# Operand tiles with a home of their own in each stage, 0 to 192 bytes further on

## The chip, the cores and the metric

The kernel runs as one program on one core of a Trainium2 chip. The metric is the device time of one execution in microseconds (us). Two executions of the kernel before took 2618.04 and 2622.47 us, median 2620.26 us.

## The reference, cut to what matters

The program computes two small networks one after the other, all in float32, on 256 tokens of width 1024.

```python
# first block: two layers on x (256 latents) and ctx (256 context tokens)
x = x + 0.5 * gt1 * swiglu(modulate(x, g1, sh1, sc1), ffn1_wi[i], ffn1_wo[i])   # same for ctx
y = conformer_conv(...)          if i == 0      # pointwise, 31 taps, LayerNorm, pointwise
y = windowed_gqa_sink(...)       if i == 1
x = x + gt2 * y
x = x + 0.5 * gt3 * swiglu(modulate(x, g3, sh3, sc3), ffn2_wi[i], ffn2_wo[i])
x = rmsnorm(x, final_g)
# second block: two layers on x alone
h = h + mixer_ab(rms(h)) or mixer_nsa(rms(h))   # attention
h = h + swiglu(rms(h), w_ffn_gate, w_ffn_up, w_ffn_down)                        # hidden 2816
h = h + sigmoid(rms(h) @ w_ple_gate) * (p[i] @ w_ple_proj)
```

Nearly all the arithmetic is products of a weight matrix with 1024 or 2816 rows by a few hundred token columns: six feed-forward layers, the projections around the convolution and around three attentions, and the modulation vectors `silu(c) @ ada_w`. Their weights are read once.

## The kernel before, in words

**A weight slab.** The weights come from HBM in slabs of 1 MB: 128 partitions by 2048 floats, which are 8 tiles in k (128 input rows each) of 256 output columns. The sync engine loads them in turn into two slots of `raw`. ScalarE rounds a slab to float32r in `whi` (line 774), VectorE takes the remainder `raw - whi` in `wlo` (line 1308), each in halves of 1024 floats.

**An operand tile.** The tokens stand on the free axis: `hhi[p, k, t]` is the rounded normalised activation of channel `128 k + p` of token `t`, `hlo` its remainder. Both are `[128, 8, 512]` float32r. Their writers are the norm stages, the convolution and, for a late norm, the residual stage ahead of it. `ghi` and `glo` are the same for the 2816 gated channels, `[128, 22, 512]`; `ohi` and `olo`, `[128, 8, 256]`, hold the output of an attention.

**A product.** `split_mm` (lines 1853 to 1857) makes three matmuls for each tile of 128 output rows: `whi` by `hi`, `whi` by `lo`, `wlo` by `hi`. In each the 128x128 weight tile is loaded into the array (a LDWEIGHTS of its own in the trace, engine PEld) and the 512 or 256 token columns of the operand are streamed through it. `tiles_of` runs it over the 8 k tiles and 2 output tiles of a slab: 48 matmuls. So the moving operand is always one row of an operand tile, and the weight tile of the next matmul is loaded while this one streams. `tokens_of` and `value_step` turn that round: `hhi` is loaded as the weights and `whi` streams.

**The stages**, in the order of the program: three feed-forward layers on 512 columns (`up`, 22 slabs, then `down`, 12 slabs, which reads `ghi` and `glo`), of which between the first and the second stand `pw1` (8 slabs, 512 columns), the convolution on TensorE, ScalarE and VectorE, and `pw2` (4 slabs, 512 columns). In the three `up` stages the matmuls of the modulation (line 1932, 32 columns of weights) stand between the slabs. Then on 256 columns: `qkv` (its fifth slab on 512), attention, `wo` (4 slabs, reads `ohi`), `up`, `down`; `qknorm` (8 slabs), attention, `wo`, `up`, `down`, `pleproj`, `plegate` (4 slabs); `nsa` (11 slabs), attention, `wo`, `up`, `down`, `pleproj`, `plegate`.

**What sets the order.** Each engine has its own program, written out by hand from a plan of stages, with counting semaphores between them. The trace's lines of interest: 1855 to 1857 (the three matmuls), 774 and 1308 (the split of the slab), 1392, 1399 and 1517 (`hlo`), 1932 (modulation), 1907 to 1909 and 2283 to 2285 (`hhi` as weights).

**Where the tiles lie.** The tiles are laid out in the order in which they are declared. In bytes of a partition, and past the last multiple of 256:

| tile | start, before | past 256, before |
|---|---|---|
| `hhi` / `hlo` | 32896 / 49280 | 128 / 128 |
| `whi` / `wlo` | 82048 / 98432 | 128 / 128 |
| `ghi` / `glo` | 136000 / 181056 | 64 / 64 |
| `ohi` / `olo` | 136000 / 144192 | 64 / 64 |
| `uhi` / `ulo` (convolution, moving) | 195264 / 202144 | 192 / 160 |
| `diag_hi` / `diag_lo` (convolution, weights) | 170688 / 182976 | 192 / 192 |

A row of an operand tile is 2048 bytes, a weight tile 512 bytes in a row of 1024, so within a stage the remainders of 256 are the same for every k tile.

Of the kernel before, what the change touches and what calls it, by code (L numbers as in the profile page):

```python
# [21 lines left out]
P = 128  # L22
# [107 lines left out]
class Stage:  # L130


    def __init__(self, kind, slabs=0, T=S, mod=None, layer=0, ada=0, gate=None, how=None, gain=None, what=None):
        self.kind, self.slabs, self.T, self.mod, self.layer = kind, slabs, T, mod, layer
        self.ada, self.gate, self.how, self.gain, self.what = ada, gate, how, gain, what
        self.late, self.feeds, self.norm, self.both, self.direct = False, None, None, False, False
        self.next_norm, self.carried = None, False


def ffn_stages(layer, tokens, ada=0, mod=None):  # L140

    return [Stage("up", 22, T=tokens, ada=ada), Stage("down", 12, T=tokens, mod=mod)]


def make_plan():
# [45 lines left out]
    for i, norm in enumerate(st):  # L191
        if norm.kind == "norm" and st[i - 1].kind == "plegate":
            st[i - 1].next_norm, norm.carried = norm, True
        if norm.kind == "norm" and not norm.late:
            j = i - 1
            while st[j].kind == "mods":
                j -= 1
            if st[j].kind in ("down", "pw2", "wo"):

                st[j].direct = norm.direct = True  # L200
                st[j:i] = st[j + 1:i] + [st[j]]
    return st

# [119 lines left out]
def build(nc, slabs_d, x_d, vec_d, const_d, w2_d, tab_d, hot_d, rope_d, mask_d, p_d, out_d, stop_after=None):  # L323
# [10 lines left out]
    with ExitStack() as ctx:  # L334
# [53 lines left out]
        with ExitStack() as at:  # L388
# [30 lines left out]
        phi, plo = hhi[:, 0:2, S:2 * S], hlo[:, 0:2, S:2 * S]  # L419
        pp = x[:, :, S:2 * S]  # L420
# [103 lines left out]

        block = ctx.enter_context(nc.Block())

        def x_final(eng, st):
# [231 lines left out]
        def _(act):  # L759
# [74 lines left out]
            def up_late(st):  # L834
                n, m = st.n0, st.m0
                with act.Fori(0, 11) as i:

# [9 lines left out]
            def up(st):  # L847
                if st.late:
                    up_late(st)
                    return  # L850
                both = st.ada // 2
                act.wait_ge(lines_done, 16)
                for first, count, ada in ((0, both, True), (both, 11 - both, False)):
# [21 lines left out]
            def residual(st):  # L875
                ks = st.slabs // 4

                def last_squares(m):
# [50 lines left out]
            def norm(st):  # L929
# [5 lines left out]
                if not st.summed:  # L935
                    preload(ACT.Sqrt)
                x_final(act, st)
                if st is not opening:
# [83 lines left out]
            def conv(st):  # L1022

                x_final(act, st)
                u_high(6)
# [231 lines left out]

            def pleload(st):
                act.wait_ge(p_landed, 16 * (st.layer + 1))
                nc.scalar.activation(phi, ptok[:, :, :], ACT.Copy).then_inc(p_split, 1)  # L1260
# [37 lines left out]
        def _(dve):  # L1298
# [73 lines left out]
            def norm(st):  # L1372
                if st.late:
                    inverse(st)
                    return
                x_final(dve, st)
                if st is not opening:
                    inverse(st)
# [39 lines left out]
            def up_late(st):  # L1418
                n, m = st.n0, st.m0
                a, b = acc[:, m % 2, :, 0:S], acc[:, (m + 1) % 2, :, 0:S]  # L1420
                scale = across(rs[:, 0:S], 2)
                dve.wait_ge(rs_ready, st.rs0)
                with dve.Fori(0, 11) as i:
# [18 lines left out]
            def up(st):  # L1442
                if st.late:
                    up_late(st)
                    return
                both = st.ada // 2
                for first, count, ada in ((0, both, True), (both, 11 - both, False)):
                    if not count:
# [19 lines left out]
            def residual(st):  # L1468

                ks = st.slabs // 4  # L1470
                xf = x[:, :, :].rearrange("p a b -> p (a b)")
                mGf = mG[:, :, :, :].rearrange("p a b c -> p (a b c)")
# [107 lines left out]
            def conv(st):  # L1580

                u_low(6)
                u_low(7)
# [237 lines left out]

            def pleload(st):
                dve.wait_ge(p_split, 2 * st.layer + 1)
                nc.vector.tensor_tensor(plo, ptok[:, :, :], phi.bitcast(F32), ALU.subtract).then_inc(p_split, 1)
# [27 lines left out]
        def _(pe):  # L1852
# [18 lines left out]
            def tiles_of(n, m, op, T, i=0, per=0, k0=0, nk=SLAB_K, first=True, last=True, paced=None,  # L1871
                         mid=None, operand=None):


                for k in range(nk):
# [5 lines left out]
                    if paced:  # L1881
                        pe.wait_ge(h_ready, paced.h0 - paced.made + paced.made * (k + 1) // DT)
                    if operand and k0 + k in operand[1]:
                        pe.wait_ge(operand[0], operand[1][k0 + k])
                    for t in range(2):
# [5 lines left out]

            def tokens_of(n, m, count, cols=SLAB_N, i=0, per=0, behind_first=None):

                for tt in range(count):
                    if tt == 1 and behind_first:
# [127 lines left out]
            def half_pair(st, c, n, m, i, per):  # L2023

                slab_there(n, i, per)
                set_free(m, i, 2)
                tiles_of(n, m, (hhi, hlo), st.T, i, per, paced=st if c == 0 else None).then_inc(slab_used, 1)

            def up_late(st):
                n, m = st.n0, st.m0  # L2030
                slab_there(n)
                set_free(m)
                tiles_of(n, m, (hhi, hlo), S, paced=st, mid=st.norm).then_inc(slab_used, 1)
                half_pair(st, 1, n + 1, m + 1, 0, 2)
                with pe.Fori(0, 10) as i:
                    for c in range(2):
                        slab_there(n + 2 + c, i, 2)
                        set_free(m + 2 + c, i, 2)
                        tiles_of(n + 2 + c, m + c, (hhi, hlo), S, i, 2).then_inc(slab_used, 1)

# [33 lines left out]
            def residual(st):  # L2074
                ks = st.slabs // 4
                operand = None
                if st.kind == "down":
                    op, operand = (ghi, glo), (g_lo, {0: st.g0, HT - 2: st.g0 + 1})
                elif st.kind == "wo":
                    made = 2 + 8 * st.att0  # L2080
                    op, operand = (ohi, olo), (o_lo, {0: made - 1, DT - 1: made})
                else:
                    op = (hhi, hlo)
                with pe.Fori(0, 2) as i:
                    for c in range(2):
                        m = st.m0 + c
                        set_free(m, i, 2)
                        for kk in range(ks):
# [4 lines left out]
                                     paced=st if st.kind == "pw2" and c == 0 else None,  # L2093
                                     operand=operand if c == 0 else None).then_inc(slab_used, 1)

# [32 lines left out]
            def qkv(st):  # L2128
# [8 lines left out]
                for c in range(6):  # L2137
# [3 lines left out]
                    if c < 5:  # L2141
                        ins = tiles_of(n, m, (hhi, hlo), S if c < 4 else 2 * S, paced=st if c == 0 else None)
                    else:
                        ins = tokens_of(n, m, 4, behind_first=lambda: rotated(4))
                    ins.then_inc(slab_used, 1)
# [3 lines left out]
            def qknorm(st):  # L2149
                n, m = st.n0, st.m0  # L2150
                with pe.Fori(0, st.slabs // 2) as i:
                    for c in range(2):
                        slab_there(n + c, i, 2)
                        set_free(m + c, i, 2)
                        tiles_of(n + c, m + c, (hhi, hlo), S, i, 2, paced=None if c else st).then_inc(slab_used, 1)
                    for c in range(2):
# [5 lines left out]
            def nsa(st):  # L2162
# [6 lines left out]
                def tiles(p):  # L2169
                    there(p)  # L2170
                    tiles_of(n + p, m + p, (hhi, hlo), S, paced=st if p == CK else None).then_inc(slab_used, 1)

# [6 lines left out]
                def hidden(kv):  # L2179
                    pe.wait_ge(mlp_landed[kv], 16)  # L2180
                    pe.wait_ge(cmp_dve, kv + 1)
                    for k in range(16):
                        ins = nc.tensor.matmul(B[3 * kv][:, 0:64], mlp[:, kv, P * k:P * k + P], blk[:, kv, k, :],
                                               start=(k == 0), stop=(k == 15))
                    ins.then_inc(hid_done, 1)

                def gate_tiles():
# [35 lines left out]
                there(V0)  # L2223
                tokens_of(n + V0, m + V0, 2).then_inc(slab_used, 1)
                pe.wait_ge(cmp_dve, 4)
# [18 lines left out]
                there(V1)  # L2244
                tokens_of(n + V1, m + V1, 2).then_inc(slab_used, 1)

            def att(st):
                A0 = 32 * st.att0
                win, nsa = st.what == "window", st.what == "nsa"
                ab = st.what == "ab"  # L2250
                if ab:
                    x_final(pe, st)
# [124 lines left out]
            def pleproj(st):  # L2377

                pe.wait_ge(p_split, 2 * st.layer + 2)
                slab_there(st.n0)  # L2380
# [12 lines left out]
            def plegate(st):  # L2393
                for c in range(4):
                    slab_there(st.n0 + c)
                    set_free(st.m0 + c)
                    tiles_of(st.n0 + c, st.m0 + c, (hhi, hlo), S, paced=None if c else st).then_inc(slab_used, 1)
                    if st.next_norm and c:
# [124 lines left out]
```

## Time and profile before

| | |
|---|---|
| two executions | 2618.04 and 2622.47 us, median 2620.26 |
| the profiled execution, first to last instruction | 2621.3 us |
| TensorE matmul busy | 2505.4 us, 96% |
| TensorE weight load busy | 2139.4 us, 82% |
| VectorE busy | 1336.2 us, 51% |
| ScalarE busy | 1155.1 us, 44% |
| mean granted TensorE clock | 0.973 |
| data moved | 374.88 MB, 143 GB/s |

The profiled execution has no time of its own beside the span; its span lies between the two times and 1.0 us above their median. Busy is the union of the recorded lengths. The length of a matmul in the trace (389 ns) is longer than the distance to the next one (227 ns), since matmuls are pipelined; what a matmul costs a stream is the distance from start to start.

### The profile page before, as it was taken

Reading aid. Unit: us, or ns where it says so; the run is one execution under the profiler, and the core shown is the slowest. Engines: PE = TensorE matmul, PEld = TensorE weight load, DVE = VectorE, ACT = ScalarE, POOL = GpSimd, SP = SyncE. Lnnn points to the kernel's source line nnn. Section 1 sums busy time; section 2 is a strip of 40 time slices with the busy share of each in tenths; the row PEclk is TensorE's granted clock in tenths of the full one; section 3 lists DMA queues with packets and bytes.
Section 4 is the critical chain, followed back from the end, with each engine's and each line's share of the span. In section 5 each row is a group of like instructions: output and inputs, shape, how many; then the busy total and the mean of one; then the engine's idle time right before and its main releaser. Section 6 shows DMA issues by size and latency. Waiting matters only on the chain.

```text
span 2621.3 us, 39926 instructions
## 1 busy us (share of the span) xinstructions
PE 2505.4 (96%) x15799; PEld 2139.4 (82%) x15799; DVE 1336.2 (51%) x2003; ACT 1155.1 (44%) x1827; POOL 23.7 (1%) x37
## 2 busy tenths in 40 slices
PE   6999999998999999999999998999889998979998
PEld 4777787875777778777788777999869998869998
DVE  4323334896523233422333466555777665776665
ACT  3323323464433322332322356554556555565554
POOL 0000000000000000000000000000100001000000
PEclk8999999999999999999999999999999998999999
DMA  7444542210344442244423221445424455403554
GB/s 312 167 161 170 186 172 88 89 49 1 114 181 170 161 159 96 104 185 160 170 102 112 82 96 65 176 176 193 166 79 177 180 194 196 157 34 116 189 188 150
DMA packets 52724, 374.88 MB, mean 143 GB/s; under 512 B 5822, under 2 KB 7034, under 8 KB 8736
## 3 DMA queue, kind: packets, MB, share of 16 engines
q1 hardware_dynamic: 50000, 358.63, 37.0%
q0 software_dynamic: 2208, 14.37, 1.6%
q8 instruction: 55, 0.90, 0.1%
q10 hardware_dynamic: 432, 0.73, 0.1%
q14 instruction: 29, 0.24, 0.0%
HBM read 372.55 MB, written 7.39 MB: 145 GB/s over the span
## 4 chain that ended last, share of the span: by engine, by line
PE 89%; DVE 6%; ACT 2%; issue 1%; DMA 1%; SPq 0%; ACTq 0%; DVEq 0%
PE acc L1855 27%; PE acc L1856 26%; PE acc L1857 26%; PE bank L1932 3%; DVE wlo L1308 1%; PE bank L1959 1%; DMA ada_raw<-in_slabs 1%; PE acc L2352 1%; DVE prod L598 1%; DVE sc L1757 1%; PE acc L2326 1%; PE bank L1990 1%; DVE prod L1674 0%; PE Mod L1942 0%; DVE hlo L1392 0%
## 5 line engine op out<-in xcount | busy, mean ns | idle before, releaser
L1308 DVE TENSOR_TENSOR wlo<-raw,whi 128x1024 fp32r<-128x1024 f32 x534 | 646.0, 1223 | 901.4 <-ACT whi L774 900.9
L774 ACT ACTIVATE whi<-raw 128x1024 fp32r<-128x1024 f32 x534 | 556.2, 1055 | 969.8 <-PE acc L1857 912.5
L1855 PE MATMUL acc<-hhi,whi 128*128 128x256 f32 (+1 forms) x2808 | 949.1, 338 | 30.0 <-DVE hlo L1392 13.2
L1856 PE MATMUL acc<-hlo,whi 128*128 128x256 f32 (+1 forms) x2808 | 935.2, 333 | 0.0
L1857 PE MATMUL acc<-hhi,wlo 128*128 128x256 f32 (+1 forms) x2808 | 934.9, 333 | 0.0
L1855 PEld LDWEIGHTS acc<-hhi,whi 128*128 128x128 f32 x2808 | 538.8, 192 | 115.0 <-issue 58.6
L1857 PEld LDWEIGHTS acc<-hhi,wlo 128*128 128x128 f32 x2808 | 538.7, 192 | 50.3
L1856 PEld LDWEIGHTS acc<-hlo,whi 128*128 128x128 f32 x2808 | 539.2, 192 | 49.7 <-issue 1.7
L1855 PE MATMUL acc<-ghi,whi 128*128 128x512 f32 (+1 forms) x1056 | 354.5, 336 | 0.0
L1856 PE MATMUL acc<-glo,whi 128*128 128x512 f32 (+1 forms) x1056 | 354.3, 336 | 0.0
L1857 PE MATMUL acc<-ghi,wlo 128*128 128x512 f32 (+1 forms) x1056 | 354.3, 336 | 0.0
L1855 PEld LDWEIGHTS acc<-ghi,whi 128*128 128x128 f32 x1056 | 198.2, 188 | 24.1
L1857 PEld LDWEIGHTS acc<-ghi,wlo 128*128 128x128 f32 x1056 | 198.2, 188 | 24.0
L1856 PEld LDWEIGHTS acc<-glo,whi 128*128 128x128 f32 x1056 | 198.2, 188 | 24.0
L1460 DVE TENSOR_TENSOR prod<-gate_sb,acc 128x1024 f32<-128x1024 f32 (+1 forms) x44 | 47.9, 1088 | 111.8 <-PE acc L1857 111.8
L1543 DVE SCALAR_TENSOR_TENSOR v<-ubuf,vec,v 128x512 f32<-128x512 f32 x150 | 100.0, 757 | 0.0
L1932 PE MATMUL bank<-raw,cwin 128*32 128x256 f32 x992 | 69.0, 398 | 1.1 <-issue 1.1
L958 ACT ACTIVATE hhi<-prod,mB 128x256 fp32r<-128x256 f32 x88 | 43.2, 506 | 35.6 <-DVE prod L598 35.5
L1855 PE MATMUL acc<-ohi,whi 128*128 128x256 f32 x192 | 54.5, 284 | 0.3 <-DVE olo L1792 0.3
L1856 PE MATMUL acc<-olo,whi 128*128 128x256 f32 x192 | 54.2, 282 | 0.0
L860 ACT ACT_TABLE_LOAD x42 | 53.9, 1283 | 0.7
L1857 PE MATMUL acc<-ohi,wlo 128*128 128x256 f32 x192 | 54.2, 282 | 0.0
(286 smaller groups left out, 2201.1 us busy)
## 6 DMA issues: line engine op xcount, KB each, us to landing
raw<-in_slabs SPq DMA_DIRECT2D x329, 1024.0 KB, 4.8
ada_raw<-in_slabs SPq DMA_DIRECT2D x10, 1024.0 KB, 26.1
skew_dram<-lines_dram POOLq DMA_DIRECT2D x1, 6144.0 KB, 23.7
bt<-skew_dram POOLq DMA_DIRECT2D x4, 1024.0 KB, 9.4
x<-in_x_in SPq DMA_DIRECT2D x1, 2048.0 KB, 17.8
mlp<-in_slabs POOLq DMA_DIRECT2D x2, 1024.0 KB, 6.1
out<-x SPq DMA_DIRECT2D x1, 1024.0 KB, 4.8
rope<-in_rope POOLq DMA_DIRECT2D x1, 512.0 KB, 4.0
```

The source lines that it names most:

```text
L598: return engine.scalar_tensor_tensor(dst, x[:, c, cols], g, r[:, cols], ALU.mult, ALU.mult)
L774: nc.scalar.activation(whi[:, n % 2, cols], raw_of(n, cols), ACT.Copy).then_inc(ready, 1)
L860: nc.scalar.activation(junk_act[:, :], eps[:, :], ACT.Silu)
L958: ins = nc.scalar.activation(dst, ub[:, k % 4, :], ACT.Identity, bias=mB[:, st.mod, c, s:s + 1])
L1308: nc.vector.tensor_tensor(wlo[:, n % 2, cols], raw_of(n, cols), whi[:, n % 2, cols].bitcast(F32), ALU.subtract).then_inc(low, 1)
L1460: nc.vector.tensor_tensor(prod[:, :, 0:T], gate_sb[:, :, 0:T], acc[:, (m + 1) % 2, :, 0:T], ALU.mult).then_inc(acc_free[(m + 1) % 2], 1)
L1543: nc.vector.scalar_tensor_tensor(tile, ub2[:, 2 * j:2 * j + 2, t:t + S], vec[:, w:w + 1], tile, ALU.mult, ALU.add).then_inc(conv_dve, 1)
L1757: ins = nc.vector.tensor_tensor_reduce(probs(st, v)[:, keys * s:keys * s + keys], B[v % 4][:, keys * s:keys * s + keys], bias, 1.0, LOWEST ...
L1855: nc.tensor.matmul(out, w[0], xx[0], start=first, stop=False)
L1856: nc.tensor.matmul(out, w[0], xx[1], start=False, stop=False)
L1857: return nc.tensor.matmul(out, w[1], xx[0], start=False, stop=last)
L1932: ins = nc.tensor.matmul(ada_bank(st, a // 2)[32 * j:32 * j + 32, 0:SLAB_N], cwin[:, k, at:at + 32], src[:, k * SLAB_N:(k + 1) * SLAB_N], ...
```

## The change: what it does

Each of `hhi`, `hlo`, `ghi` and `glo` becomes a flat buffer, 64 floats (256 bytes) longer for the first two and 32 floats (128 bytes) longer for the others. A stage sees its operand tile as a window in that buffer that begins at the stage's home. A home is a number of floats, a pair for (hi, lo) of `hhi` and `hlo`, one number for `ghi` and `glo`. The writer of an operand and its readers take the same home. Two small tiles, `kcsq` and `kcr`, give their room and become parts of `arow`.

```diff
+ROOM, G_ROOM = 64, 32
+HOMES = dict(up=((16, 16), (32, 32), (48, 48), (16, 16), (32, 32), (8, 8)), pw1=((8, 8),), conv=((0, 16),),
+             qkv=((16, 0),), qknorm=((8, 8),), plegate=((32, 32), (8, 8)), nsa=((48, 48),))
+G_HOMES = (16, 8, 32, 16, 8, 32)
+
+def place_operands(plan):
+    left = {kind: list(homes) for kind, homes in HOMES.items()}
+    home, g_home, ups = (0, 0), 0, 0
+    for i, st in enumerate(plan):
+        if st.kind in ("norm", "conv"):
+            reader = st.kind if st.kind == "conv" else plan[i + 1].kind
+            home = left[reader].pop(0)
+        if st.kind == "up":
+            g_home = G_HOMES[ups]
+            ups += 1
+        st.home, st.g_home = home, g_home
...
-        hhi = sb("hhi", [P, DT, 2 * S], F32R)
-        hlo = sb("hlo", [P, DT, 2 * S], F32R)
+        hhi_all = sb("hhi", [P, DT * 2 * S + ROOM], F32R)
+        hlo_all = sb("hlo", [P, DT * 2 * S + ROOM], F32R)
...
-            ghi = sb("ghi", [P, HT, 2 * S], F32R, ffn)
-            glo = sb("glo", [P, HT, 2 * S], F32R, ffn)
+            ghi_all = sb("ghi", [P, HT * 2 * S + G_ROOM], F32R, ffn)
+            glo_all = sb("glo", [P, HT * 2 * S + G_ROOM], F32R, ffn)
...
-            kcsq = sb("kcsq", [P, 64], F32, at)
-            kcr = sb("kcr", [P, 64], F32, at)
...
+        kcsq, kcr = arow[:, 0, 0:64], arow[:, 0, 64:128]
...
+        def operand(st):
+            return tuple(a[:, at:at + DT * 2 * S].rearrange("p (a t) -> p a t", t=2 * S)
+                         for a, at in zip((hhi_all, hlo_all), st.home))
...
+        def gated_operand(st):
+            return tuple(a[:, st.g_home:st.g_home + HT * 2 * S].rearrange("p (a t) -> p a t", t=2 * S)
+                         for a in (ghi_all, glo_all))
...
-                tiles_of(n, m, (hhi, hlo), st.T, i, per, paced=st if c == 0 else None).then_inc(slab_used, 1)
+                tiles_of(n, m, operand(st), st.T, i, per, paced=st if c == 0 else None).then_inc(slab_used, 1)
```

The homes that result, in bytes, in the order of the stages:

| stage (columns) | `hhi` | `hlo` | `ghi` and `glo` |
|---|---|---|---|
| first `up`, `down` (512) | 64 | 64 | 64 |
| `pw1` (512) | 32 | 32 | |
| `pw2` (512) | 0 | 64 | |
| second `up`, `down` (512) | 128 | 128 | 32 |
| third `up`, `down` (512) | 192 | 192 | 128 |
| `qkv` (256, one slab 512) | 64 | 0 | |
| fourth `up`, `down` (256) | 64 | 64 | 64 |
| `qknorm` (256) | 32 | 32 | |
| fifth `up`, `down`, `pleproj`, `plegate` (256) | 128 | 128 | 32 |
| `nsa` (256) | 192 | 192 | |
| sixth `up`, `down`, `pleproj`, `plegate` (256) | 32 | 32 | 128 |

With the longer buffers `hlo` starts 256 bytes later than before, `whi`, `wlo`, `ghi`, `ohi` and all that follows 512 bytes later, `glo` 640 bytes later. So against `whi` and `wlo`, modulo 256, `hhi`, `hlo` and `ghi` move by their home alone and `glo` by its home and 128; `ohi`, `olo` and the tiles of the convolution stay as they were. The instructions of each engine, their sizes, their order and their waits are the same as before, but for the names `kcsq` and `kcr`.

## Rows read from the trace of the kernel before

**Rows 1.** The page: busy by engine, granted clock in 40 slices, end chain.

```profile
PE 2505.4 (96%) x15799; PEld 2139.4 (82%) x15799; DVE 1336.2 (51%) x2003; ACT 1155.1 (44%) x1827; POOL 23.7 (1%) x37
...
PEclk8999999999999999999999999999999998999999
...
PE 89%; DVE 6%; ACT 2%; issue 1%; DMA 1%; SPq 0%; ACTq 0%; DVEq 0%
```

**Rows 2.** Groups by shape: names, count, busy us, mean ns, idle before.

```profile
L1855 PE MATMUL acc<-hhi,whi 128*128 128x512 f32 x1264 | 502.8, 398 | 17.5 <-DVE hlo L1601 7.4 <-DVE hlo L1392 6.6 <-issue 3.6
L1855 PE MATMUL acc<-hhi,whi 128*128 128x256 f32 x1544 | 446.3, 289 | 12.5 <-DVE hlo L1392 6.6 <-DVE hlo L1399 5.8
L1855 PE MATMUL acc<-ghi,whi 128*128 128x512 f32 x528 | 208.7, 395 | 0.0
L1855 PE MATMUL acc<-ghi,whi 128*128 128x256 f32 x528 | 145.8, 276 | 0.0
...
L1907 PE MATMUL acc<-whi,hhi 128*128 128x256 f32 x64 | 20.4, 318 | 0.8 <-DVE wlo L1308 0.8
```

**Rows 3.** Stretches by stage: span, PE, PEld, DVE, ACT, POOL, clock, DMA, GB/s.

```profile
452.00:541.00 89.00, 89.00 (x384) 73.27 (x383) 76.32 (x117) 45.11 (x91) 0.00 (x0) 0.97 0.27 95
...
1982.00:2109.00 127.00, 127.00 (x1057) 126.89 (x1057) 84.30 (x91) 78.67 (x94) 0.00 (x0) 1.00 0.51 186
2109.00:2169.00 60.00, 60.00 (x531) 60.00 (x530) 36.88 (x40) 28.51 (x34) 0.00 (x0) 1.00 0.53 202
2200.00:2276.00 76.00, 68.87 (x522) 65.86 (x521) 49.97 (x54) 45.39 (x72) 12.92 (x16) 0.91 0.50 180
...
2583.00:2621.00 38.00, 30.09 (x246) 29.46 (x245) 21.50 (x25) 16.70 (x22) 0.00 (x0) 0.95 0.31 111
```

**Rows 4.** TensorE in order of time, `hhi`, 512 columns: first and 28th.

```profile
299.85 0.39 PE L1855 MATMUL acc<-hhi,whi 128*128 128x512 f32 x1
...
305.97 0.39 PE L1855 MATMUL acc<-hhi,whi 128*128 128x512 f32 x1
```

**Rows 5.** The same, `ghi`, 512 columns: first and 19th.

```profile
323.63 0.39 PE L1856 MATMUL acc<-glo,whi 128*128 128x512 f32 x1
...
327.83 0.39 PE L1856 MATMUL acc<-glo,whi 128*128 128x512 f32 x1
```

**Rows 6.** The same, convolution, 512 columns: first and 27th.

```profile
569.83 0.40 PE L1855 MATMUL acc<-uhi,diag_hi 128*128 128x512 f32 x1
...
575.90 0.39 PE L1857 MATMUL acc<-uhi,diag_lo 128*128 128x512 f32 x1
```

**Rows 7.** The same, `hhi`, 256 columns: first and 19th.

```profile
1699.74 0.28 PE L1857 MATMUL acc<-hhi,wlo 128*128 128x256 f32 x1
...
1701.90 0.28 PE L1857 MATMUL acc<-hhi,wlo 128*128 128x256 f32 x1
```

**Rows 8.** The same, `ghi`, 256 columns: first and 20th.

```profile
1779.81 0.28 PE L1856 MATMUL acc<-glo,whi 128*128 128x256 f32 x1
...
1781.96 0.28 PE L1857 MATMUL acc<-ghi,wlo 128*128 128x256 f32 x1
```

**Rows 9.** The same, `ohi`, 256 columns: first and 20th.

```profile
1614.78 0.28 PE L1855 MATMUL acc<-ohi,whi 128*128 128x256 f32 x1
...
1616.94 0.28 PE L1856 MATMUL acc<-olo,whi 128*128 128x256 f32 x1
```

**Rows 10.** The same, `hhi`, 512 columns, at the half clock: first and fourth.

```profile
48.53 0.63 PE L1857 MATMUL acc<-hhi,wlo 128*128 128x512 f32 x1
...
49.81 0.63 PE L1857 MATMUL acc<-hhi,wlo 128*128 128x512 f32 x1
```

More of the change, by code:

```diff
@@ L835, in up_late @@
                 n, m = st.n0, st.m0
+                ghi, glo = gated_operand(st)
                 with act.Fori(0, 11) as i:
@@ L851, in up @@
                 both = st.ada // 2
+                ghi, glo = gated_operand(st)
                 act.wait_ge(lines_done, 16)
@@ L876, in residual @@
                 ks = st.slabs // 4
+                hhi, hlo = operand(st.feeds or st)
                 def last_squares(m):
@@ L936, in norm @@
                     preload(ACT.Sqrt)
+                hhi, hlo = operand(st)
                 x_final(act, st)
@@ L1022, in conv @@
             def conv(st):
+                hhi, hlo = operand(st)
                 x_final(act, st)
@@ L1376, in norm @@
                 x_final(dve, st)
+                hhi, hlo = operand(st)
                 if st is not opening:
@@ L1421, in up_late @@
                 scale = across(rs[:, 0:S], 2)
+                ghi, glo = gated_operand(st)
                 dve.wait_ge(rs_ready, st.rs0)
@@ L1446, in up @@
                 both = st.ada // 2
+                ghi, glo = gated_operand(st)
                 for first, count, ada in ((0, both, True), (both, 11 - both, False)):
@@ L1470, in residual @@
                 ks = st.slabs // 4
+                hhi, hlo = operand(st.feeds or st)
                 xf = x[:, :, :].rearrange("p a b -> p (a b)")
@@ L1580, in conv @@
             def conv(st):
+                hhi, hlo = operand(st)
                 u_low(6)
@@ L1890, in tiles_of, with tokens_of @@
                 return ins
-            def tokens_of(n, m, count, cols=SLAB_N, i=0, per=0, behind_first=None):
+            def tokens_of(n, m, op, count, cols=SLAB_N, i=0, per=0, behind_first=None):
+                hhi, hlo = op
                 for tt in range(count):
@@ L2032, in up_late @@
                 set_free(m)
-                tiles_of(n, m, (hhi, hlo), S, paced=st, mid=st.norm).then_inc(slab_used, 1)
+                tiles_of(n, m, operand(st), S, paced=st, mid=st.norm).then_inc(slab_used, 1)
                 half_pair(st, 1, n + 1, m + 1, 0, 2)
@@ L2038, in up_late @@
                         set_free(m + 2 + c, i, 2)
-                        tiles_of(n + 2 + c, m + c, (hhi, hlo), S, i, 2).then_inc(slab_used, 1)
+                        tiles_of(n + 2 + c, m + c, operand(st), S, i, 2).then_inc(slab_used, 1)
             def up(st):
@@ L2141, in qkv @@
                     if c < 5:
[L2142 removed]
+                        ins = tiles_of(n, m, operand(st), S if c < 4 else 2 * S, paced=st if c == 0 else None)
                     else:
[L2144 removed]
+                        ins = tokens_of(n, m, operand(st), 4, behind_first=lambda: rotated(4))
                     ins.then_inc(slab_used, 1)
@@ L2154, in qknorm @@
                         set_free(m + c, i, 2)
-                        tiles_of(n + c, m + c, (hhi, hlo), S, i, 2, paced=None if c else st).then_inc(slab_used, 1)
+                        tiles_of(n + c, m + c, operand(st), S, i, 2, paced=None if c else st).then_inc(slab_used, 1)
                     for c in range(2):
@@ L2170, in tiles @@
                     there(p)
-                    tiles_of(n + p, m + p, (hhi, hlo), S, paced=st if p == CK else None).then_inc(slab_used, 1)
+                    tiles_of(n + p, m + p, operand(st), S, paced=st if p == CK else None).then_inc(slab_used, 1)
                 def head_sums(p):
@@ L2185, in hidden @@
                     ins.then_inc(hid_done, 1)
+                hhi, hlo = operand(st)
                 def gate_tiles():
@@ L2250, in att @@
                 ab = st.what == "ab"
+                hhi, hlo = operand(st)
                 if ab:
@@ L2396, in plegate @@
                     set_free(st.m0 + c)
-                    tiles_of(st.n0 + c, st.m0 + c, (hhi, hlo), S, paced=None if c else st).then_inc(slab_used, 1)
+                    tiles_of(st.n0 + c, st.m0 + c, operand(st), S, paced=None if c else st).then_inc(slab_used, 1)
                     if st.next_norm and c:
```

29 lines of the change are left out of this document (18 added, 11 removed).

## The prediction

> **What bounds the kernel now.** I read the page first. TensorE is busy for 96% of the span, the chain that ended last runs through it for 89%, and the granted clock is full nearly everywhere [rows 1]. So the question is what one matmul costs in the stream. The change touches nothing but the place of its operand, and the groups by shape say how many there are: line 1855 is one of three equal lines, so `hhi` and `hlo` stream 3 x 1264 = 3792 times with 512 columns and 3 x 1544 = 4632 times with 256, `ghi` and `glo` 3 x 528 = 1584 times with each [rows 2]. The stretches by stage show that inside a stage nothing else limits: TensorE is busy for 89.00 of 89, 127.00 of 127 and 60.00 of 60 us while VectorE and ScalarE have room, though VectorE is at 76 of 89 us in `pw1` [rows 3].
>
> Then the starts in order of time give the price. From start to start:
>
> | operand, columns | rows | price, ns | columns at 2.4 GHz, ns | loss, ns | operand against weights, modulo 256 |
> |---|---|---|---|---|---|
> | `hhi`, 512 | [rows 4], 6.12 us / 27 | 226.7 | 213.3 | 13.4 | 0 bytes |
> | `ghi`, 512 | [rows 5], 4.20 us / 18 | 233.3 | 213.3 | 20.0 | 192 |
> | conv, 512 | [rows 6], 6.07 us / 26 | 233.5 | 213.3 | 20.2 | many (4 bytes per tap) |
> | `hhi`, 256 | [rows 7], 2.16 us / 18 | 120.0 | 106.7 | 13.3 | 0 |
> | `ghi`, 256 | [rows 8], 2.15 us / 19 | 113.2 | 106.7 | 6.5 | 192 |
> | `ohi`, 256 | [rows 9], 2.16 us / 19 | 113.7 | 106.7 | 7.0 | 192 |
>
> Same line, same shape, same clock, and the price differs by 6 to 7 ns with the tile that streams. That is what this change can move. The last column comes from the table of addresses: `hhi` lies 128 past a multiple of 256 as `whi` does, `ghi` and `ohi` 64 past. The sign is what I want the reader to see: being level with the weights is the better place at 512 columns and the worse one at 256. A further sign that weight load and stream disturb each other: at half clock the same matmul costs 1.28 us / 3 = 426.7 ns, which is 512 columns at 1.2 GHz with no loss at all [rows 10]. There the stream goes at half its full pace.
>
> **The change part by part.** No instruction, size or wait is added or removed, so each term is a count times a difference of two prices.
>
> *512 columns, moved whole.* The three `up` stages (22 slabs x 48 = 1056 each, 3168) and `pw1` (8 x 48 = 384) are 3552 matmuls. Their new distances are 64, 128, 192 and 32 bytes. One of them, 192, has a row (233.3); the convolution walks over many others and comes to 233.5, which is the nearest evidence for 32, 64 and 128. I take 233.3 for all: 3552 x 6.6 ns = +23.4 us. Bounds: 213.3 (no loss, as at half clock) and 240 (a loss once more as large over the level place).
>
> *512 columns, moved in part.* `pw2` moves only `hlo`, one matmul of three (64 of 192), and the one 512 slab of `qkv` only `hhi`, two of three (32 of 48): 96 x 6.6 ns = +0.6 us.
>
> *256 columns, moved whole.* Three `up` (3168), `qknorm` (384), the tile slabs of `nsa` (8.5 x 48 = 408), two `plegate` (384) and two `pleproj` (96) are 4440 matmuls, at distances 64, 32, 192, 128 and 32. Two rows off the level place give 113.2 and 113.7, both at 192, and no row tells of 32, 64 or 128. I take 113.3 for all, 6.7 ns less: -29.7 us. Bounds: 106.7 (no loss) and 126.7 (the loss grows by as much as it could fall).
>
> *256 columns, in part.* `qkv` moves two of three of 192: 128 x 6.7 = -0.9 us. `hhi` as weights (line 1907 and the two after it, 64 each [rows 2]) would win 192 x 6.7 = -1.3 us; the same in the attention of `mixer_ab` stands between waits and is taken at nothing.
>
> *What is lost of it.* In the stretch of `nsa` TensorE is busy for 68.87 of 76 us and in the last `plegate` for 30.09 of 38 [rows 3]: it waits there for steps that do not get shorter. I take half of the 408 + 192 matmuls as hidden: 300 x 6.7 = +2.0 us.
>
> *`ghi` and `glo`.* The new distances of (`ghi`, `glo`) are (0, 128), (224, 96) and (64, 192) bytes, once each with 512 and with 256 columns. Only the first makes two of three matmuls level: 352 x 6.6 ns less at 512 and 352 x 6.7 more at 256, which is 0. The others stay off level, 0.
>
> *The writers, the two small tiles, the slabs.* ScalarE and VectorE write at starts that remain multiples of 32 bytes, and TensorE waits for `hlo` only 26 us in all (7.4 + 6.6 + 6.6 + 5.8, lines 1601, 1392 and 1399 [rows 2]); 0. `kcsq` and `kcr` in `arow` have the waits that they had, 0. Faster 256-column slabs need faster slabs from HBM: 48 x 113.3 ns is 5.4 us each, and `down` takes 12 slabs in 60 us, 5.0 us each, with TensorE never idle [rows 3]. That cover holds.
>
> Sum: +23.4 + 0.6 - 29.7 - 0.9 - 1.3 + 2.0 = -5.9 us, against the profiled execution's 2621.3 us: 2615.4. That execution is 1.0 us over the median, so **2614 us**. The change is small because two tariffs nearly cancel, not because nothing happens.
>
> **A rule that speaks against it.** Prices at one shape differ by 6 to 7 ns between tiles [rows 7, 8]. The Trainium skill ("TensorE: Matmul & The Clock Gate", Part 2, step-by-step) says that TensorE has two independent read ports into SBUF and that loading the next weights takes no bandwidth from the running matmul, and gives N / 2.4 + 2.5 ns from start to start; by that every `hhi` matmul would cost 215.8 or 109.2 ns, at any address. This case's trace disagrees with the figures (226.7 and 120.0).
>
> **The rivals.**
>
> *1. Placement modulo 256 is not the cause.* The tiles that differ in price also differ in region: `hhi` lies below `whi`, while `ghi`, `ohi` and `uhi` lie above it. If region sets the price, or anything that 32 bytes do not change, nothing moves: 2620. For: no row has one tile at two places. Against: a loss that differs between 512 and 256 columns in opposite directions looks like two address streams meeting, and a far region has no reason to help one and harm the other. Beside this stands the Trainium skill ("SBUF — State Buffer", the box on cachelines): lines of 16 bytes and a price for crossing them. All homes are multiples of 32 bytes, so by that rule too the time stays at 2620.
>
> *2. Off level is better everywhere.* 192 may be the one bad distance at 512 columns, and the convolution's figure may come from its two-piece rows. Then 512-column matmuls fall to 220.0, by one step of 6.7: 3552 x -6.7 = -23.8; with -29.9 from the 256-column terms and `ghi` and `glo` at 226.7 instead of 233.3 with 512 columns (1584 x -6.6 = -10.5) the time is 2556. The milder form, 512 as it is and 256 lower, gives 2590. For: homes of 32 to 128 bytes are untried in the trace. Against: over 26 convolution matmuls at changing distances the mean is the 233.5 of the bad place.
>
> *3. The 512-column price rises and the 256-column one does not fall.* If only 192 bytes gives 113.3 at 256 columns, then of the moved stages `nsa` alone gains, some 1 us, and the rest stay at 120. With 512 columns at 233.3 that is +24 - 1: 2643; at 236 (9.3 ns over, 3552 of them) 2653. It decides from the point where the 256-column saving is under 24.0 / 4440 = 5.4 ns each. For: only one distance off level is priced at 256 columns. Against: nothing in the rows.
>
> **How the numbers follow.** Forecast 0.39, rival 1 0.19, rival 2 0.21 (a third of it in the strong form), rival 3 0.21. The forecast's own range is 2598 to 2630: a fifth of the moved matmuls in either class at the other price. To hold 8 in 10 the range takes in rival 1, the milder rival 2 (2590, with a little below it) and rival 3 up to 2648: **2580 to 2648**. Two per cent, about what a measurement can tell from no change, is 52 us here: 2568 and 2673. Faster by more needs the strong rival 2: 0.07. Slower by more needs rival 3 with the 256-column price up a step as well (+24 + 30 us): 0.04. Within: 0.89.
>
> **What the changed profile would show.** Start to start in the first three `up` stages: 233 if the term is right, 227 for rival 1, 220 or less for rival 2. In the fourth `up`: 113 if right, 120 for rivals 1 and 3. `nsa` at 113 is the surest number, for it has the distance of `ghi` before. In the first `down` two of three matmuls level with the weights should bring 233 towards 229, and in the fourth `down` 113 towards 118. `ohi` and the convolution must read as before. What would make it wrong: a price that depends on how far hi and lo lie from each other, or on the distance modulo 512, since `hlo` moved by 256 against `hhi` and the trace before never separated those; and waits at the ends of stages that grow when the matmuls get quicker.

## The result and the profile after

The changed kernel takes 2637.64 us (2637.38 and 2637.91) against 2620.26 before: ratio on record 1.0058, 95% interval 1.0037 to 1.008. The ratio makes it 15.2 us slower, the two medians 17.4 us (their quotient is 1.0066); with two executions of each kernel the two agree within the interval. That is inside the stated range of 2580 to 2648 and inside 2%, but above no change, where 2614 was forecast: the sign was wrong.

The page of the changed kernel, the lines that answer to [rows 1]:

```profile
span 2635.2 us, 39926 instructions
PE 2524.0 (96%) x15799; PEld 2143.7 (81%) x15799; DVE 1336.7 (51%) x2003; ACT 1155.8 (44%) x1827; POOL 23.7 (1%) x37
...
PE 89%; DVE 6%; ACT 2%; issue 1%; DMA 1%; SPq 0%; ACTq 0%; DVEq 0%
```

TensorE is busy 18.6 us longer, VectorE and ScalarE within 1 us as before. The groups by shape of the changed kernel (line 1855 is now 1903), to be held against [rows 2]:

```profile
L1903 PE MATMUL acc<-hhi,whi 128*128 128x512 f32 x1264 | 510.0, 404 | 15.1 <-DVE hlo L1648 7.4 <-DVE hlo L1435 4.2 <-DVE wlo L1350 3.6
L1903 PE MATMUL acc<-hhi,whi 128*128 128x256 f32 x1544 | 442.5, 287 | 12.8 <-DVE hlo L1435 6.7 <-DVE hlo L1442 5.8
```

The recorded 512-column matmul became longer (398 to 404 ns), the 256-column one shorter (289 to 287). The waits ahead of them moved little, from 17.5 to 15.1 us and from 12.5 to 12.8. By stage, the stretches that answer to [rows 3] (columns as there, ends cut at whole us):

```profile
454.00:546.00 92.00, 91.38 (x383) 72.82 (x384) 77.32 (x120) 45.85 (x92) 0.00 (x0) 0.98 0.26 92
...
2000.00:2126.00 126.00, 126.00 (x1061) 125.90 (x1060) 84.68 (x92) 79.01 (x94) 0.00 (x0) 1.00 0.53 186
2126.00:2188.00 62.00, 62.00 (x532) 62.00 (x532) 37.47 (x41) 28.52 (x34) 0.00 (x0) 1.00 0.54 199
```

`pw1` takes 92 us instead of 89, the fifth `up` 126 instead of 127, the fifth `down` 62 instead of 60; from first start to last they are 2.3 us longer, 1.4 shorter and 1.9 longer. Now the starts in order of time in the changed kernel, as in [rows 4] to [rows 9]. Each pair is the first and the last of 19 (first `up`) or 31 matmuls: `hhi` with 512 columns in the first `up` (home 64 bytes), `pw1` (32) and the third `up` (192).

```profile
102.22 0.39 PE L1903 MATMUL acc<-hhi,whi 128*128 128x512 f32 x1
...
106.34 0.39 PE L1903 MATMUL acc<-hhi,whi 128*128 128x512 f32 x1
...
469.66 0.40 PE L1904 MATMUL acc<-hlo,whi 128*128 128x512 f32 x1
...
476.66 0.40 PE L1904 MATMUL acc<-hlo,whi 128*128 128x512 f32 x1
...
1199.78 0.39 PE L1904 MATMUL acc<-hlo,whi 128*128 128x512 f32 x1
...
1206.78 0.39 PE L1904 MATMUL acc<-hlo,whi 128*128 128x512 f32 x1
```

4.12 / 18 = 228.9 ns, 7.00 / 30 = 233.3 and again 233.3, where 226.7 stood. With 256 columns: the fifth `up` (128 bytes), the sixth (32) and the fourth `down`.

```profile
2049.75 0.28 PE L1903 MATMUL acc<-hhi,whi 128*128 128x256 f32 x1
...
2053.31 0.28 PE L1903 MATMUL acc<-hhi,whi 128*128 128x256 f32 x1
...
2449.82 0.28 PE L1904 MATMUL acc<-hlo,whi 128*128 128x256 f32 x1
...
2453.32 0.28 PE L1904 MATMUL acc<-hlo,whi 128*128 128x256 f32 x1
...
1799.78 0.28 PE L1904 MATMUL acc<-glo,whi 128*128 128x256 f32 x1
...
1803.31 0.28 PE L1904 MATMUL acc<-glo,whi 128*128 128x256 f32 x1
```

118.7, 116.7 and 117.7 ns. The first two were 120.0 and were forecast at 113.3; the last was 113.3 before and was forecast to rise towards 118.

Below, a price is the mean over a whole stage of the distances from start to start under 140 ns (256 columns) or 260 ns (512). The lengths of the stages, from first start to last, add the difference up: 512-column `hhi` stages +16.7 us, 256-column `hhi` stages -8.4, `ghi` and `glo` -1.5 with 512 columns and +6.6 with 256; together +13.4 of the 13.9 us between the spans.

### The profile page after: what moved, and what is told of

It is laid out like the page before. It is cut to its first block, busy times and chain, and to the rows that moved or that the text cites. A ratio compares the mean times of both kernels' runs of the same rounds, so it can differ in the third digit from the quotient of the medians.

```text
span 2635.2 us, 39926 instructions
## 1 busy us (share of the span) xinstructions
PE 2524.0 (96%) x15799; PEld 2143.7 (81%) x15799; DVE 1336.7 (51%) x2003; ACT 1155.8 (44%) x1827; POOL 23.7 (1%) x37
## 4 chain that ended last, share of the span: by engine, by line
PE 89%; DVE 6%; ACT 2%; issue 1%; DMA 1%; SPq 0%; ACTq 0%; DVEq 0%
PE acc L1903 27%; PE acc L1904 26%; PE acc L1905 26%; PE bank L1981 3%; PE bank L2008 1%; DVE wlo L1350 1%; DMA ada_raw<-in_slabs 1%; PE acc L2404 1%; PE acc L2378 1%; DVE sc L1804 1%; DVE prod L634 1%; PE bank L2039 1%; DVE prod L1721 0%; PE Mod L1991 0%; ACT pT L1260 0%
## 5 line engine op out<-in xcount | busy, mean ns | idle before, releaser
L953 ACT ACTIVATE gate_sb<-x 128x512 f32<-128x512 f32 (+1 forms) x34 | 26.4, 776 | 63.2 <-DVE x L1550 63.2
```

What stands on the lines that cost most here:

```text
L953: ins = nc.scalar.activation(sq[:, :, 0:st.T], x[:, bass.ds(2 * c + 4 * i, 2), 0:st.T], ACT.Square, scale=ROOT_EPS if st.both else 1.0)
```

## The experiments

Distances are bytes by which the moving operand lies past the weights, modulo 256. Level means 0 bytes off. Theory A is the forecast's. The first four kernels ran once each, beside one run of the kernel before at 2622.05 us: their traces carry the argument, their times do not.

**The homes back to 0.** The first suspect was the longer buffers: `hlo` now lies 256 bytes later against `hhi`.

```diff
-HOMES = dict(up=((16, 16), (32, 32), (48, 48), (16, 16), (32, 32), (8, 8)), pw1=((8, 8),), conv=((0, 16),),
+HOMES = dict(up=((0, 0),) * 6, pw1=((0, 0),), conv=((0, 0),), ...)     # all (0, 0)
-G_HOMES = (16, 8, 32, 16, 8, 32)
+G_HOMES = (80, 96, 112, 80, 96, 112)     # with 256 floats of room behind ghi: glo level with ghi
```

> The changed kernel with the homes of hhi and hlo all 0; the longer buffers stay, so against the weights hhi stands 512 bytes off and hlo 768 bytes off, both 0 modulo 256. ghi and glo are level with each other modulo 1024 and stand 0, 64 and 128 bytes off the weights, once each with 512 and with 256 columns. Theory A (only the distance modulo 256 sets the price, as forecast): every up stage reads as before, 226.8 ns at 512 columns and 120.0 at 256; ghi at 0 bytes 227 and 120, at 64 and 128 bytes 233 and 113. Theory B (the period is longer than 256 bytes, or the distance between hi and lo counts): the up stages do not return to 226.8 and 120.0, they read 229 to 233 and 116 to 119 as in the changed kernel. Theory C (region, not distance): ghi reads 233 and 113 at all three.

2630.51 us. All six `up` stages went back to their prices of before, 227.2 to 227.4 and 120.0. In order of time, `hhi` with 256 columns, `ghi` level with the weights with 512 and then with 256 columns, each the first and last of 31:

```profile
1999.80 0.28 PE L1904 MATMUL acc<-hlo,whi 128*128 128x256 f32 x1
...
2003.40 0.28 PE L1904 MATMUL acc<-hlo,whi 128*128 128x256 f32 x1
...
349.81 0.39 PE L1904 MATMUL acc<-glo,whi 128*128 128x512 f32 x1
...
356.61 0.39 PE L1904 MATMUL acc<-glo,whi 128*128 128x512 f32 x1
...
1789.79 0.28 PE L1905 MATMUL acc<-ghi,wlo 128*128 128x256 f32 x1
...
1793.38 0.28 PE L1905 MATMUL acc<-ghi,wlo 128*128 128x256 f32 x1
```

120.0, 226.7 and 119.7 ns (120.0 over the whole stage). So 512 and 768 bytes are the same place as 0, and `ghi` costs what `hhi` costs once it lies as `hhi` does. Theory B falls for the level place and theory C (region) falls altogether: the same tile in the same region went from 233.3 to 226.7 and from 113.4 to 120.0. But `ghi` at 64 and 128 bytes read 117.8 and 118.7 at 256 columns, not 113, and at 64 bytes 228.9 at 512, not 233. There is the forecast's error.

**The change's homes, hi and lo level modulo 1024.**

```diff
         hhi_all = sb("hhi", [P, DT * 2 * S + ROOM], F32R)
+        # const, mA, mB, mG, two_gains here: 768 bytes modulo 1024
         hlo_all = sb("hlo", [P, DT * 2 * S + ROOM], F32R)
+        # vec, gb, spare, neg_sink, rs_tok here: the same
...
-G_HOMES = (16, 8, 32, 16, 8, 32)
+G_HOMES = (0, 16, 32, 0, 16, 32)         # ghi and glo 192, 0 and 64 bytes off
```

> The changed kernel's homes, but with small tiles placed between the big ones so that hhi, hlo and whi are level modulo 1024 at home 0, as before the change; a stage's home is now its true distance for hi and lo alike. ghi, glo and ohi stand 192 bytes off modulo 1024 (704 before), ghi and glo with homes of 0, 64 and 128 bytes more. Theory A (modulo 256): the same prices as in the changed kernel, since modulo 256 nothing differs: up 229.2, 232.2, 233.4 at 512 columns, 117.8, 118.7, 116.7 at 256. Theory B (longer period, hi against lo): the prices differ from the changed kernel's by over 1 ns in several stages, and those with 192 bytes come to 233.3 and 113.4. For ohi: 113.4 if 192 and 704 are the same place (period 512 or 256), another price if the period is 1024.

2629.21 us. The `up` stages read 229.0, 232.3, 233.3 and 117.8, 118.7, 116.7, as in the changed kernel to 0.1 ns: the period is 256 bytes there too. Three numbers were not theory A's. `nsa`, at 192 bytes, reads 113.3 over its longest unbroken stretch where the changed kernel has 117.8; `ohi`, at 192 bytes as ever, reads 117.8 three times, where it had 113.4; and the sixth `down`, at 64 bytes, reads 113.3, where `ghi` at 64 read 117.8 in the kernel before this one. That `ohi` went from 704 to 192 bytes modulo 1024 is not the cause: at 704 it reads 117.8, 117.8 and 113.5 in the kernel with the homes at 0, and at 192 it reads both 113.4 and 117.8 in the later ones.

**Everything moved together** (the kernel before, with 64 unused bytes ahead of `hhi`):

```diff
+        front_pad = sb("front_pad", [P, 16])
         hhi = sb("hhi", [P, DT, 2 * S], F32R)
```

> The kernel before with 64 unused bytes ahead of hhi: every tile behind x lies 64 bytes further on, all distances between operands and weights stay. If only distances count: 226.8 and 120.0 in the up stages, 233.3 and 113.4 in the down stages, time as before, 2620 us within 0.3%. If a tile's own address counts (the start within a line or a bank): prices move by over 1 ns.

2622.11 us. All prices stayed within 0.6 ns, except the second `ohi` stage, 117.8 instead of 113.4. So for a shift of 64 bytes, which as a distance costs 2 ns, the address itself does not count.

**hi and lo apart**, in the layout of the kernel with hi and lo level:

```diff
+HOMES = dict(up=((0, 16), (0, 32), (0, 64), (0, 16), (0, 32), (0, 64)), pw1=((16, 0),), ...)
+G_HOMES = (48, 80, 112, 48, 80, 112)
```

> hhi level with the weights modulo 1024 in all up stages, hlo alone 64, 128 and 256 bytes off, with 512 and with 256 columns; pw1 has hhi alone 64 bytes off, qknorm hhi alone 128 bytes off, nsa both 256 bytes off. ghi and glo together 384, 512 and 640 bytes off. Theory A (each matmul pays for its own distance modulo 256): hlo at 64 and 128 changes one matmul of three, 226.8 to about 229 and 120.0 to about 118; hlo at 256 and nsa at 256 read as before, 226.8 and 120.0; ghi at 512 reads 227 and 120. Theory B (period over 256): hlo at 256 reads otherwise than 226.8 and 120.0, and nsa at 256 otherwise than 120.0.

2632.17 us. `hlo` alone 64 bytes off costs 232.0 ns at 512 columns, more than both off by 64 (229.1); alone 128 bytes off, 232.0 and 117.8; alone 64 off at 256 columns, 120.0. Alone 256 bytes off it costs nothing (227.3, 120.0), and both 256 bytes off, in `nsa`, read 119.9. `hhi` alone 64 bytes off costs 233.3 in `pw1`, alone 128 off 119.7 in `qknorm`. So "each matmul pays for its own distance" fails: with `hlo` alone 64 bytes off, all three distances from start to start grew, to 231.4, 232.0 and 232.5 ns, where they were 226.8, 227.4 and 227.6. The change's `pw2` has this placement and the same 232.0; its first `down`, with `ghi` level and `glo` 128 bytes off, reads 233.3, not the 232.0 of `hhi` and `hlo` placed so.

**Two places only, and the kernel before once more.** The map so far says: level at 512 columns, 192 at 256.

```diff
+HOMES = dict(up=((0, 0), (0, 0), (0, 0), (48, 48), (48, 48), (48, 48)), pw1=((0, 0),), conv=((0, 0),),
+             qkv=((48, 48),), qknorm=((48, 48),), plegate=((48, 48), (48, 48)), nsa=((48, 48),))
+G_HOMES = (16, 16, 16, 0, 0, 0)          # in the level layout: 0 and 192 bytes off
```

> Level layout (hhi, hlo and whi level modulo 1024 at home 0), only two places: every stage with 512 columns has hhi, hlo, ghi and glo 0 bytes off the weights modulo 256, every stage with 256 columns has them 192 bytes off. Theory D (price by distance modulo 256, and at 256 columns off the level place one of two steady patterns, 113.4 or 117.8 ns, by the way the stream began): 226.7 in all 512-column products, which wins 1584 x 6.6 ns = 10.5 us in the three down stages; 113.4 or 117.8 in the 256-column ones that were at 120.0, 4440 x 6.6 = 29 us at best and 4440 x 2.2 = 10 us at worst. Time 2580 to 2600 us against 2621. Theory C (region): down at 512 columns stays at 233.3 and up at 256 at 120.0, 2620 us.

2593.57 us, 0.9883 of before (0.9848 to 0.9917). All `up` and `down` stages at 512 columns read 226.7 to 227.4: theory C (region) fails once more. In its trace the fourth and the fifth `up`, both 192 bytes off, first and last of 31 each:

```profile
1699.78 0.28 PE L1903 MATMUL acc<-hhi,whi 128*128 128x256 f32 x1
...
1703.18 0.28 PE L1903 MATMUL acc<-hhi,whi 128*128 128x256 f32 x1
...
1999.83 0.28 PE L1905 MATMUL acc<-hhi,wlo 128*128 128x256 f32 x1
...
2003.36 0.28 PE L1905 MATMUL acc<-hhi,wlo 128*128 128x256 f32 x1
```

113.3 and 117.7 ns: one place, one kernel, one execution, two steady prices. The price can also change inside a stage, across a break in the stream. In `nsa` of the same trace, two neighbouring slabs with a few other matmuls between them, first and last of 31 each:

```profile
2234.53 0.28 PE L1905 MATMUL acc<-hhi,wlo 128*128 128x256 f32 x1
...
2238.07 0.28 PE L1905 MATMUL acc<-hhi,wlo 128*128 128x256 f32 x1
...
2240.54 0.28 PE L1905 MATMUL acc<-hhi,wlo 128*128 128x256 f32 x1
...
2243.94 0.28 PE L1905 MATMUL acc<-hhi,wlo 128*128 128x256 f32 x1
```

118.0 and 113.3 ns. The traces of all kernels here hold some 400 unbroken 256-column streams of 30 or more matmuls; after its first 15 none goes from one of the two prices to the other. The four executions of this kernel took 2588.24 to 2605.16 us.

> The kernel before, unaltered, profiled once more. Theory D says the pattern a stream falls into at 256 columns off the level place is a matter of how it began, so ohi and ghi read 113.4 or 117.8 from one execution to the next, while hhi reads 120.0 and the 512-column stages the same figures always. If the pattern belongs to the program: 113.4 in all six, as in the first profile.

All six `ohi` and `ghi` stages at 256 columns read 113.4 again, and 2621.51 us. So the pattern came back with the program, in two executions; in three kernels with `nsa` at 192 bytes its five slab streams also read 113, 113, 118, 113 and 118 in the same order. A stream's pattern is set where it starts; which of the two it falls into is not explained by anything the traces show.

**Two maps of further distances**, with the level layout:

```diff
+HOMES = dict(up=((4, 4), (24, 24), (40, 40), (24, 24), (40, 40), (56, 56)), ...)   # first map
+HOMES = dict(up=((2, 2), (12, 12), (28, 28), (12, 12), (28, 28), (44, 44)), ...)   # second map
```

> Level layout, hi and lo together at distances that no stage had: hhi and hlo 16, 96 and 160 bytes off in the three 512-column up stages, 224 in pw1, 240 in pw2; 96, 160 and 224 in the 256-column up stages, 96 in qkv, 16 in qknorm, 240 in nsa; ghi and glo 32, 96 and 224 off at both widths. Theory D: at 512 columns all between 226.7 and 233.5, with 226.7 the floor at 0 alone; at 256 columns all between 113.4 and 120. If a better place exists, one of them reads under 226 or under 113.

> The same with hhi and hlo 8, 48 and 112 bytes off in the 512-column up stages, 176 in pw1, 144 in pw2; 48, 112 and 176 in the 256-column up stages, 48 in qkv, 208 in qknorm, 80 in nsa; ghi and glo 160, 240 and 16 bytes off at both widths. Theory D: as for the other map. A start that is no multiple of 16 bytes (8) tells whether that costs anything by itself: over 233.5 if so.

2648.13 and 2645.11 us, against 2625.38 for the kernel before. Whole-stage prices with hi and lo together, from all kernels here, in ns (most distances stand in one or two stages of one execution):

| bytes off | 512 columns | 256 columns |
|---|---|---|
| 0 | 226.7 to 227.4 (57 stages) | 119.6 to 120.0 (67) |
| 8 | 233.2 | |
| 16 | 231.5, 231.7 | 118.7, 118.7 |
| 32 | 233.3 | 116.7 to 117.8 |
| 48 | 233.3 | 118.3 |
| 64 | 228.9 to 229.2 | 117.8, once 113.3 |
| 80 | | 119.7 |
| 96 | 233.2 to 233.4 | 120.0 |
| 112 | 230.2, and 231.1 in one slab | 113.3 to 113.5 |
| 128 | 232.2 to 233.3 | 118.7, once 120.0 |
| 144 | 233.3 | |
| 160 | 234.2, 234.3 | 118.7 |
| 176 | 233.3 | 119.2 |
| 192 | 233.3 (20) | 113.3 or 117.8 (74, a few broken stages between) |
| 208 | | 119.1 |
| 224 | 233.3 | 118.3 |
| 240 | 226.7 and 236.7 | 117.2 |

`hhi` and `ghi` agree at most distances that both have. They differ at 240 with 512 columns (226.7 against 236.7), by 1 ns at 128 with 512 and at 32 with 256, and where the pattern has two prices. Theory D's bounds at 512 columns failed at 160 and at 240: over 233.5 in three stages, and at 240 once as low as the level place. No stage went under 226.7 and 113.3.

**The parts of the change, each alone**, in 4, 10 and 8 executions, beside 17 of the kernel before with a median of 2625.21 us. The edits in words:

```diff
+HOMES: only up 1 to 3, pw1, conv as in the change, rest (0, 0); ghi, glo as before    # first
+HOMES: only up 4 to 6, qkv, qknorm, plegate, nsa as in the change; ghi, glo as before  # second
+HOMES: all (0, 0); G_ROOM and G_HOMES as in the change                                # third
```

> The change's homes for hhi and hlo in the stages with 512 columns alone; the 256-column stages at home 0, ghi and glo where they were against the weights. By the stretches of the changed kernel's trace (three up stages +3.3, +4.5 and +6.3 us, pw1 +2.3, pw2 and the 512 slab of qkv included) this costs +16 to +17 us, ratio 1.006. Forecast's own term was +24. Rival (waits at the ends of stages, not prices, made it slower): under +8.

2640.51 us, 1.0061 (1.0037 to 1.0084): +16.0 us by the ratio, as in the two that follow. The third `up` of its trace, at 192 bytes, first and last of 31, 233.3 ns:

```profile
1199.83 0.40 PE L1903 MATMUL acc<-hhi,whi 128*128 128x512 f32 x1
...
1206.83 0.40 PE L1903 MATMUL acc<-hhi,whi 128*128 128x512 f32 x1
```

> The change's homes for hhi and hlo in the stages with 256 columns alone. By the stretches of the changed kernel's trace -8 us, ratio 0.997; the forecast's own term was -30, ratio 0.989. Prices 117.8, 118.7 and 116.7 ns in the three up stages if they belong to the place of the operand.

2618.74 us, 0.9981 (0.9966 to 0.9995): -5.0 us. The -8.4 us of the stages lies inside that interval (-8.9 to -1.3). The `up` stages read 117.8, 118.7 and 116.7, the very numbers of the changed kernel. Two stages fell the other way than there or than before: `nsa` reads 113.3 over its longest unbroken stretch, on the same addresses on which the changed kernel reads 117.8, and the sixth `down`, whose place did not change, reads 117.8 instead of 113.4, which costs 2.3 us. `nsa`, first and last of 31:

```profile
2226.26 0.28 PE L1905 MATMUL acc<-hhi,wlo 128*128 128x256 f32 x1
...
2229.66 0.28 PE L1905 MATMUL acc<-hhi,wlo 128*128 128x256 f32 x1
```

> The change's places for ghi and glo alone (homes 64, 32 and 128 bytes, and glo 128 bytes off ghi); hhi and hlo at home 0. By the stretches of the changed kernel's trace +5 us, of which +7 in the three down stages at 256 columns (117.8, 117.0 and 117.8 ns instead of 113.4) and -1.5 at 512; ratio 1.002. The forecast's own term was 0: 113.4 or 118 in the fourth down and 113.4 in the fifth and sixth.

2630.72 us, 1.0016 (1.0003 to 1.0029): +4.2 us, with 117.8, 117.0 and 117.8 ns in the three `down` stages at 256 columns. The three parts add up to +15.2 us, or 1.0058, the change's own ratio. That it agrees so closely is luck, since each part is known only to some 3 to 6 us.

**112 bytes instead of 192.** One `up` stage of the second map read 113.4 there.

```diff
-             qkv=((48, 48),), qknorm=((48, 48),), plegate=((48, 48), (48, 48)), nsa=((48, 48),))
-G_HOMES = (16, 16, 16, 0, 0, 0)
+             qkv=((28, 28),), qknorm=((28, 28),), plegate=((28, 28), (28, 28)), nsa=((28, 28),))
+G_HOMES = (16, 16, 16, 44, 44, 44)
```

> As the kernel with two places, with 112 bytes instead of 192 for hhi, hlo, ghi and glo at 256 columns (one up stage read 113.4 there). If 112 has the one steady pattern: 113.4 in all six up and down stages, 2583 us or 0.984 of before. If it has two, as 192: some stages at 117 to 119, 2590 to 2600 us.

2585.94 us, 0.9859 (0.9842 to 0.9876), the lowest median of all; its interval overlaps that of the kernel with 192 (0.9848 to 0.9917), so that it is faster rests on the traces, where the fifth `up` and `down` went from 117.8 to 113.4 and the `pleproj` and `plegate` behind them to 113.7. Its page, its fifth `up` (the stretch that took 127 us in [rows 3]) and the fifth `down`:

```profile
span 2581.8 us, 39926 instructions
PE 2467.7 (96%) x15799; PEld 2111.4 (82%) x15799; DVE 1334.2 (52%) x2003; ACT 1155.5 (45%) x1827; POOL 23.7 (1%) x37
```

```profile
1962.00:2082.00 120.00, 120.00 (x1056) 119.89 (x1055) 83.18 (x92) 78.93 (x94) 0.00 (x0) 1.00 0.56 194
2082.00:2142.00 60.00, 60.00 (x532) 60.00 (x531) 37.14 (x41) 28.44 (x34) 0.00 (x0) 1.00 0.55 206
```

All six `up` and `down` stages at 256 columns read 113.3 to 113.5, all 512-column ones 226.7 to 227.4, but for the one slab of `qkv` (231.1).

## Why the prediction was wrong, point by point

| term | forecast, us | measured, us |
|---|---|---|
| 512 columns, `hhi` and `hlo`, whole and in part | +24.0 | +16.7 by stages, +16.0 by the part alone |
| 256 columns, `hhi` and `hlo`, after what is lost | -29.9 | -8.4 by stages, -5.0 alone |
| `ghi` and `glo` | 0 | +5.1 by stages, +4.2 alone |
| sum | -5.9 | +13.4 by stages, +15.2 by the parts |

*The mechanism was right, as far as it went.* The price hangs on the distance between moving operand and weights modulo 256, for `hhi` and for `ghi`: level is the best place at 512 columns (226.7 ns) and no better than any other at 256 (120.0). That weight load and stream meet in some way is the prediction's reading of it and stays argued; the runs show the dependence, not its reason. Rival 1 (region, or no effect of places 32 bytes apart) is out by the homes set back and by `ghi` made level.

Two sentences of the Trainium skill stood beside the prediction. "TensorE: Matmul & The Clock Gate", Part 2, step-by-step, says that TensorE has two independent read ports, so that loading weights takes nothing from the running matmul. The runs disagree: the place of the operand alone moved the price between 226.7 and 233.3 ns, and between 120.0 and 113.3. "SBUF — State Buffer", the box on cachelines, gives lines of 16 bytes. They do not account for the prices: places of 32 and 64 bytes, both whole lines, read 233.3 and 229.1 ns.

*The step that failed* is "I take 113.3 for all, 6.7 ns less: -29.7 us". Both rows behind it were of one distance, 192, as the text said. The three `up` stages at 64, 128 and 32 bytes measured 117.8, 118.7 and 116.7: they saved 2.2, 1.3 and 3.3 ns. Over all the moved 256-column stages the saving was 8.4 us where 29.9 were forecast. The turning point named under rival 3, a saving under 5.4 ns each, was passed, and rival 3 is the case that came, in a milder form: at 256 columns most places are a little cheaper than the level one, not 6.7 ns.

*The second failure* is the term at 0 for `ghi` and `glo`. "The others stay off level, 0" took every place off level for 192. The three `down` stages at 256 columns stood at the best price seen, 113.4, and could only lose: they lost 4.4, 3.7 and 4.4 ns over 528 matmuls each, +6.6 us by stages. At 512 columns those `down` stages stood at 233.3 and won little: 230.4 in the third, and nothing in the first, where two of three matmuls were level. The term "352 x 6.6 ns less at 512" failed with it (measured 0), while its counterpart at 256 columns, 352 x 6.7 = 2.4 us more, came (2.3 us).

*Mis-sized:* 512 columns, too dear by 7 us. 233.3 came in `pw1` and the third `up`; the second `up` was 232.3, the first, at 64 bytes, 229.1. Besides, the `up` stages stood at 227.2 to 227.4 before, not at the 226.7 of one row, which is 2 of the 7 us. The convolution's 233.5 did not stand for each distance that it runs over.

*Right:* little but prices moved. Stages explain 13.4 of the 13.9 us between the spans, which leaves nothing of size for the writers, `kcsq` and `kcr` in `arow` and the waits (only `qkv` grew, by 1.2 us, while its price fell), and the cover for faster slabs held even where all of them ran at 113.3 (120.00 us busy of 120). The fourth `down` went to 118 as foretold; `ohi` and the convolution (233.0 ns on average) read as before. *Wrong among the signs:* `nsa` was called the surest number at 113 and read 117.8, since 192 bytes has two prices, and the first `down` did not leave 233.3. That the time fell inside the range is in part luck: the range was drawn for other cases, and of the three errors, +21.5 us at 256 columns, +5.1 at `ghi` and `glo` and -7.3 at 512 columns, the last took off part of the others.

## What to carry to other kernels

Where an array is fed by two streams, take the price of a matmul from start to start, by stage, and compare tiles that share line and shape: here that alone showed 3% at 512 columns and 6% at 256, unseen by any wait. A distance that is priced at one value says nothing on the others; before a layout is spread over many values, map them with one kernel whose stages each have their own, and count also what the stages stand to lose that are already at the best. Then use the few good places: level with the weights for 512 columns and 112 bytes off for 256 took 1.4% off this kernel, where the spread cost 0.6%.

## What the runs showed of the hardware that was not expected

- A stream of weight load and matmul pairs locks into a steady pattern, whose mean can be one of two at the same distance: 113.3 or 117.8 ns at 192 bytes and 256 columns, 113.3 or 117.8 at 64. At 240 bytes with 512 columns `hhi` read 226.7 and `ghi` 236.7. An unbroken stream keeps its pattern; the next one, behind a few other matmuls, can have the other. What sets it stays open: an unrelated 64 bytes ahead of all tiles changed it in one `ohi` stage.
- Whether the pattern also changes from one execution to the next is not shown. The four executions of the kernel with 192 bytes spread by 17 us and the four with 112 by 3.7, but the 17 of the kernel before, with few such stages, spread by 16 as well.
- One operand of three out of line (`hlo` by 64 bytes, 512 columns) costs more, 232.0 ns, than all in line at that distance, 229.1.
- 8 bytes off are enough to lose the level place: 233.2 ns instead of 227.2 in the first `up`.
- The best prices seen, 226.7 and 113.3 ns, are still 13.4 and 6.6 ns over the streaming time of the columns at 2.4 GHz. At half clock a matmul on the level place loses nothing, 426.7 ns [rows 10].
